# Attention's last column group computes keys first; the conformer's end runs by token half, with half of its x update inside the section

## The reference, cut to what matters

```python
# attention: three mixers on one projection of 2464 columns
proj = rmsnorm(x, ln1_g) @ w_in
qa, ka, va, cq, ckv, kr, qc, kc, vc = jnp.split(proj, split_idx, axis=-1)
out_a = mixer_dilated(qa, ka, va, ...)      # 6 heads of 64, rotary on q and k
out_b = mixer_mla(cq, ckv, kr, ...)         # 6 heads of 96
out_c = mixer_diff(qc, kc, vc, ...)         # 4 heads, two softmax maps each
x = x + jnp.concatenate([out_a, out_b, out_c], -1) @ w_o

# conformer, then x = x + rms_norm(result, g)
h = x @ w_pw1 + b_pw1
a, gate = jnp.split(h, 2, axis=-1)
h = causal_depthwise_conv(a * sigmoid(gate), w_dw) + b_dw    # 31 taps
h = silu(layernorm(h) * ln_g + ln_b)
return h @ w_pw2 + b_pw2
```

## Time and profile before

| | us |
|---|---|
| median of 3 runs | 1992.95 |
| profiled execution | 1992.19 |
| its span | 1990.4 |
| PE busy | 1945.3 (98% of the span) |
| DVE busy | 1285.6 (65%) |
| ACT busy | 970.8 (49%) |
| POOL busy | 87.0 (4%) |

### The profile page before, as it was taken

One profiled execution on the slowest core, in us unless ns is written; L12 is line 12 of the kernel. 1 busy time (PEld: TensorE's weight loads), 2 busy tenths in 40 slices (PEclk: granted clock), 3 DMA queues, 4 the chain that ended last, 5 costly groups with the idle time before them and its releaser, 6 DMA issues.

```text
span 1990.4 us, 26010 instructions
## 1 busy us (share of the span) xinstructions
PE 1945.3 (98%) x10642; PEld 1636.2 (82%) x10642; DVE 1285.6 (65%) x1649; ACT 970.8 (49%) x1251; POOL 87.0 (4%) x124
## 2 busy tenths in 40 slices
PE   6999999999999999999999999999999999999998
PEld 5768888868888887888888688889988888788887
DVE  5876565876655675676665476566765667557564
ACT  5645444655443544454455554444544453445443
POOL 0300000120000000001000000000000000000000
PEclk9999999999999999999999999999999999999999
DMA  7335654425654653566543356636566555445661
GB/s 251 127 101 175 190 190 144 170 85 185 194 191 160 222 189 127 165 202 193 191 144 120 115 187 195 191 128 210 181 211 190 190 201 190 158 154 182 190 190 63
DMA packets 197150, 340.61 MB, mean 171 GB/s; under 512 B 6757, under 2 KB 128233, under 8 KB 197032
## 3 DMA queue, kind: packets, MB, share of 16 engines
q1 hardware_dynamic: 193024, 331.04, 51.0%
q10 hardware_dynamic: 4008, 7.90, 1.2%
HBM read 337.88 MB, written 1.05 MB: 170 GB/s over the span
## 4 chain that ended last, share of the span: by engine, by line
PE 90%; DVE 6%; ACT 3%; issue 1%; DMA 0%; POOL 0%; DVEq 0%; ACTq 0%
PE ps L550 20%; PE ps L552 20%; PE ps L551 19%; PE ps L665 14%; PE ps L663 8%; PE ps L662 2%; PE ps L1066 1%; PE ps L572 1%; DVE arena L1920 1%; PE ps L1012 1%; PE ps L807 1%; PE ps L806 1%; ACT xT L1210 0%; DMA first_g<-ln_g_dram 0%; ACT arena L1359 0%
## 5 line engine op out<-in xcount | busy, mean ns | idle before, releaser
L1663 DVE TENSOR_TENSOR w_lo<-w_raw,w_hi 128x2048 fp32r<-128x2048 f32 x300 | 691.9, 2312 | 255.3 <-ACT w_hi L1158 254.8
L1158 ACT ACTIVATE w_hi<-w_raw 128x2048 fp32r<-128x2048 f32 x302 | 575.6, 1912 | 96.6 <-PE ps L552 86.2
L665 PE MATMUL ps<-xT,w_hi 128*128 128x512 f32 x1176 | 419.5, 396 | 0.0
L550 PE MATMUL ps<-w_hi,u_h 128*128 128x512 f32 (+1 forms) x1032 | 405.0, 392 | 3.9 <-DVE u_l L2124 1.8
L552 PE MATMUL ps<-w_hi,u_l 128*128 128x512 f32 (+1 forms) x1032 | 399.8, 387 | 0.0
L551 PE MATMUL ps<-w_lo,u_h 128*128 128x512 f32 (+1 forms) x1032 | 399.6, 387 | 0.0
L663 PE MATMUL ps<-xT,w_lo 128*128 128x256 f32 x1344 | 347.4, 279 | 0.0
L550 PE MATMUL ps<-w_hi,xT 128*128 128x512 f32 (+2 forms) x800 | 290.2, 363 | 9.4 <-DVE w_lo L1663 5.1
L552 PE MATMUL ps<-w_hi,xT 128*128 128x512 f32 (+2 forms) x800 | 284.2, 355 | 0.0
L551 PE MATMUL ps<-w_lo,xT 128*128 128x512 f32 (+2 forms) x800 | 284.0, 355 | 0.0
L663 PEld LDWEIGHTS ps<-xT,w_lo 128*128 128x128 f32 x1344 | 253.4, 189 | 13.6
(11 more groups left out here) (226 smaller groups left out, 1848.2 us busy)
## 6 DMA issues: line engine op xcount, KB each, us to landing
w_raw<-mlp_w_dram SPq DMA_DIRECT2D x128, 1024.0 KB, 5.4
w_raw<-ret_w_in_dram SPq DMA_DIRECT2D x48, 1024.0 KB, 5.1
w_raw<-w_up_dram SPq DMA_DIRECT2D x32, 1024.0 KB, 5.6
w_raw<-w_down_dram SPq DMA_DIRECT2D x32, 1024.0 KB, 4.8
w_raw<-w_in_dram SPq DMA_DIRECT2D x16, 1024.0 KB, 5.3
w_raw<-ret_w_out_dram SPq DMA_DIRECT2D x16, 1024.0 KB, 4.8
w_raw<-cf_w_pw_dram SPq DMA_DIRECT2D x12, 1024.0 KB, 5.4
w_raw<-sc_w_in_dram SPq DMA_DIRECT2D x12, 1024.0 KB, 5.2
```

The source lines that it names most:

```text
L550: pe.matmul(dst, lh, rh, start=start, stop=False)
L665: ins = pe.matmul(ps[:, bank, :], w_hi[:, slot, wsl], both, start=False, stop=kc == KC - 1)
L1158: act.activation(w_hi[:, slot, :], w_raw[:, slot, :], ACT.Copy).then_inc(hi_ready[slot], 1)
L1663: tt(w_lo[:, slot, :], w_raw[:, slot, :], w_hi[:, slot, :].bitcast(F32), ALU.subtract).then_inc(lo_ready[slot], 1)
```

## The change

In attention the second group's fillers (stages 8 to 15) are turned round: `late_chunk` multiplies the 256 key columns over all 8 row blocks in stages 8 to 11, two blocks a stage, then the 256 value columns in stages 12 to 15. Keys are taken out of PSUM in stage 11, values in stage 15. DVE rotates the first group in stages 9 and 10 (POOL no longer does) and the late keys in stage 14. `LATE` and its empty stage go; there are 24 stages. `out_chunk` takes token half 0 first. The splitting of one tile moves by one stage.

In the conformer up(tile 3) goes ahead of conv 0 and up(tile 5) ahead of conv 2, and the 7 `keep_busy` go. Conv 6 and 7 run as two token halves each. Everything behind them runs for half 0 and then half 1; `keep_busy` there runs 3 and 2 times. ACT has one silu of a single column ahead of the norm. The x update of half 0 (`add`, `sum_added`) is inside the section, the splitting of tiles 9 + 3 and 10 + 3 behind it, and `feed_x` of half 0 stands ahead of the last step of half 1.

```diff
-STAGES, LATE = MAPS + 5, 16
+STAGES, TURN_C = MAPS + 4, 15
...
+                def late_chunk(i):
+
+                    for kc in (2 * (i % 4), 2 * (i % 4) + 1):
+                        c, first = LATE_TILE + kc // 4, kc % 4 * 512 + 256 * (i // 4)
+                        slot = tile_ready(sec, c)
+                        for t in range(NT):
+                            ins = wide_part(sec, c, t, kc, 256, slice(first, first + 256), 2 * (i // 4) + t, 0, kc == 0, kc == KC - 1)
+                        if i >= 4 and kc % 4 == 3:
+                            ins.then_inc(used[slot], 1)
+                        elif i == 3 and kc == KC - 1:
+                            ins.then_inc(late_k.sem, 1)
...
                     if k == 0 and cc == 0:
-                        n = 4 if t == 1 else 5
+                        n = 5 + t
                         pe.wait_ge(evac_a.sem, evac_a.at(sec, n))
...
+                        if s == 12:
+                            pe.wait_ge(evac_a.sem, evac_a.at(sec, 4))
+                            pe.wait_ge(evac_v.sem, evac_v.at(sec, 4))
+                        late_chunk(s - 8)
...
-                def conv(c):
+                def conv(c, tok=slice(0, S)):
+                    bank = c % 4 - tok.start // 64
                     if c == 0:
-                        keep_busy(3, 7)
...
+                def back_late(t):
+                    for c in range(4, KC):
+                        ins = back(c, t)
+                    ins.then_inc(conv_T.sem, 1)
...
                 up(sec, 6, 2, lambda: turn_ups(sec, 1, cwide, lambda: pe.wait_ge(wu_sb.sem, wu_sb.at(sec, 2))))
+                up(sec, 7, 3)
                 conv(0)
                 conv(1)
-                up(sec, 7, 3)
                 pe.wait_ge(glu_done.sem, glu_done.at(sec, 1))
                 up(sec, 4, 4)
+                up(sec, 5, 5)
                 conv(2)
                 conv(3)
-                up(sec, 5, 5)
                 pe.wait_ge(glu_done.sem, glu_done.at(sec, 2))
                 up(sec, 6, 6)
...
+                conv(6, slice(0, P))
+                conv(7, slice(0, P))
+                conv(6, slice(P, S))
+                pe.wait_ge(conv_a.sem, conv_a.at(sec, 8))
+                back_late(0)
+                conv(7, slice(P, S))
+                pe.wait_ge(conv_a.sem, conv_a.at(sec, 10))
+                back_late(1)
...
+                def out_half(t, k):
+
+                    slot = tile_ready(sec, 8 + k)
+                    pe.wait_ge(feed_lo.sem, feed_lo.at(sec, 4 * t + k + 1))
+                    if t == 1 and k == 3:
+                        then(False)
+                    for cc in range(2):
+                        lh, ll = half_step(u_h, k)[:, cc, :], half_step(u_l, k)[:, cc, :]
...
+                keep_busy(0, 3)
+                pe.wait_ge(y_normed.sem, y_normed.at(sec, 1))
+                for k in range(4):
+                    turn_half(0, k)
+                keep_busy(0, 2)
+                out_half(0, 0)
+                out_half(0, 1)
                 pe.wait_ge(y_normed.sem, y_normed.at(sec, 2))
                 for k in range(4):
-                    if k >= 2:
-                        pe.wait_ge(feed_lo.sem, feed_lo.at(sec, k - 1))
-                    turn_step(sec, k, ch, k)
-                    if k == 1:
-                        keep_busy(3, 2)
-                    if 1 <= k < 3:
-                        down(sec, k - 1, 7 + k, first=k == 1)
-                last_downs(sec, 2, 10, then, True)
+                    turn_half(1, k)
+                out_half(0, 2)
+                out_half(0, 3)
+                for k in range(4):
+                    out_half(1, k)
+                then(True)
 
             def sc(prev, sec, then):
...
+                    if s == 11:
+                        act.wait_ge(late_k.sem, late_k.at(sec, 1))
+                        act.activation(pr[:, 0, 512:VA], ps[:, 0, 0:256], ACT.Copy, scale=rstd[:, 0:1]).then_inc(evac_a.sem, 1)
+                    if s == 15:
+                        act.wait_ge(used[sec.slot(LATE_TILE + 1)], sec.fill(LATE_TILE + 1) + 1)
+                        act.activation(pr[:, 0, VA:1024], ps[:, 2, 0:256], ACT.Copy, scale=rstd[:, 0:1]).then_inc(evac_a.sem, 1)
...
+                def high(t, k):
+                    n = 4 * t + k
+                    act.wait_ge(feed_T.sem, feed_T.at(sec, n + 3 if k < 2 else n + 1))
+                    if t == 1:
+                        act.wait_ge(feed_lo.sem, feed_lo.at(sec, k + 1))
...
+                    if t == 1 and k < 3:
+                        act.wait_ge(out_first.sem, out_first.at(sec, k + 1))
+                    elif t == 1:
+                        act.wait_ge(acc_ready.sem, acc_ready.at(sec, 2))
+                    act.activation(half_step(u_h, k), half_step(csl, k), ACT.Copy).then_inc(feed_hi.sem, 1)
+
+                act.activation(st[:, 8:9], mhalf[:, 0:1], ACT.Silu)
+                norm(0)
+                high(0, 0)
+                high(0, 1)
+                norm(1)
+                high(0, 2)
+                high(0, 3)
+                for k in range(3):
+                    high(1, k)
+                sum_added(sec, 0)
+                high(1, 3)
+                prepare(sec, 9)
+                prepare(sec, 10)
 
...
-                pool.wait_ge(rope_b.sem, rope_b.at(sec, 1))
-                pool.wait_ge(evac_a.sem, evac_a.at(sec, 4))
-                pool.wait_ge(evac_v.sem, evac_v.at(sec, 4))
-                for t in range(NT):
-                    ins = rotate(pool, step, pr[:, t, 0:512].rearrange("p (h d) -> p h d", d=AD), 512 // AD, AD // 2,
-                                 rope[:, t, 0:32], rope[:, t, 32:64], rope_pa, rope_pb)
...
+                    if s in (9, 10):
+                        t = s - 9
+                        vec.wait_ge(evac_a.sem, evac_a.at(sec, 4))
+                        vec.wait_ge(evac_v.sem, evac_v.at(sec, 4))
+                        ins = rotate(vec, step, pr[:, t, 0:512].rearrange("p (h d) -> p h d", d=AD), 512 // AD, AD // 2,
+                                     c64[t], s64[t], rope_va, rope_vb)
...
+                    if s == 14:
...
+                def low(t, k):
+                    vec.wait_ge(feed_hi.sem, feed_hi.at(sec, 4 * t + k + 1))
+                    tt(half_step(u_l, k), half_step(csl, k), half_step(u_h, k).bitcast(F32), ALU.subtract).then_inc(feed_lo.sem, 1)
+
+                statistics(0)
+                shift(0)
+                statistics(1)
+                low(0, 0)
+                shift(1)
+                for k in range(1, 4):
+                    low(0, k)
+                for k in range(3):
+                    low(1, k)
                 vec.wait_ge(bias_in.sem, bias_in.at(sec, 16))
+                add(sec, 0)
+                low(1, 3)
+                prepare(sec, 9)
+                prepare(sec, 10)
```

More of the change, by code:

```diff
@@ L930, in attn @@
                             values_pair(e)
-                    if turn and s == LATE + 1:
-                        turn_block(map_at(s))
                     filler(s)
@@ L1092, in cf @@
                 ins.then_inc(conv_T.sem, 1)
-                conv(6)
-                conv(7)
-                pe.wait_ge(conv_a.sem, conv_a.at(sec, KC))
-                for t in range(NT):
-                    for c in range(4, KC):
-                        ins = back(c, t)
-                    ins.then_inc(conv_T.sem, 1)
-                keep_busy(0, 8)
+                conv(6, slice(0, P))
+                conv(7, slice(0, P))
+                conv(6, slice(P, S))
+                pe.wait_ge(conv_a.sem, conv_a.at(sec, 8))
@@ new lines, in out_half @@
+                def out_half(t, k):
[5 more added lines that the diff above has]
+                        lh, ll = half_step(u_h, k)[:, cc, :], half_step(u_l, k)[:, cc, :]
+                        for h in range(2):
+                            wsl = slice(cc * D + h * 512, cc * D + h * 512 + 512)
+                            ins = three(ps[:, 2 * t + h, :], lh, ll, w_hi[:, slot, wsl], w_lo[:, slot, wsl],
+                                        k == 0 and cc == 0, k == 3 and cc == 1)
+                            if k == 3 and cc == 1 and not (t == 1 and h == 1):
+                                ins.then_inc(acc_ready.sem, 1)
+                    if t == 1:
+                        ins.then_inc(used[slot], 1)
+                    elif k < 3:
+                        ins.then_inc(out_first.sem, 1)
@@ L1439, in cf, with conv_out @@
             def cf(prev, sec):
-                def conv_out(c):
-                    act.wait_ge(conv_e.sem, conv_e.at(sec, c + 1))
-                    act.activation(ccv[:, c, :], ps[:, c % 4, 0:S], ACT.Identity, bias=gain("bdw", 0, c)).then_inc(conv_a.sem, 1)
+                def conv_out(c, n, tok=slice(0, S)):
+                    act.wait_ge(conv_e.sem, conv_e.at(sec, n))
```

(13 more changed lines are left out.)

121 lines of the change are left out of this document (59 added, 62 removed).

## The result

The changed kernel takes 1977.34 us, the median of four runs (1976.71 to 1978.84). The kernel before took 1992.76 in the runs beside it (1992.49 to 1993.24). The ratio is 0.9925, with a 95% interval of 0.9913 to 0.9937: 15.4 us faster. The forecast was 1981.0 us: 11.8 us off the profiled execution's 1992.19, and 0.76 more for the step from that execution to the median. The profiled execution after has a span of 1975.4 us, 15.0 shorter, and a mean granted clock of 1.000 where it was 0.998.

A forecast was written before the change was run, and what follows sets the result against it. PE bounds the kernel (busy 1945.3 of 1990.4 us), so only its idle time, half clock and empty work can be won. 4.8 + 2.4 + 1.4 + 3.2 = 11.8 us off 1992.19, plus 0.76 to the median: 1981.0, range 1976 to 1988.

The forecast's parts named there:

- Attention, PE's own work: Attention: 48 matmuls of 512 columns become 96 of 256 per layer, costing +0.5 us per layer, ends 0 and +1.
- POOL off: Attention, ninth stage: without POOL's contention DVE's maxima come 2.3 us earlier and PE's 1.64 us wait goes.
- DVE's new load: Attention: DVE's own rotations (4.2 us) and late keys (2.6) give back PE's early gain; map 16's scores start at 117.2.
- Attention, the sum: Attention: 2.8 us won in the first layer, 1.3 in the second; 3.2 taken for both, ends -3 and +6.
- The half clock: First attention, behind the late rotation: PE at 1.2 GHz for most of 120 to 123 us, about 1.5 us lost.
- The two filled waits: Conformer, ahead of conv 0 and conv 2: up(tile 3) and up(tile 5) fill waits, 4.8 us won, ends 3.9 and 4.8.
- The section's middle: Conformer, conv 6 to first output matmul: token halves take 14.1 us against 16.56, 2.4 us won.
- The x update: Conformer's end: half 0's update hides behind remaining output matmuls, the 1.18 wait goes; 1.4 us won, ends 0 and 1.9.
- (a): Conformer rival: weight loads set the floor, so a 128-token conv instruction costs what 256 tokens do; 1987 us, chance 0.10.
- (b): Attention rival: DVE is the bound throughout, PE waits 2 us more per layer, clock falls once; 1986.5 us, chance 0.15.
- (c): Conformer rival: half convs' loads run one after another at 110 ns, +20 us; 2001 us, chance 0.04.
- (d): Better case: half convs cost exactly half and attention keeps no wait but DVE's last; 1977 us, chance 0.06.

The follow-up runs named there:

- rot_only: The kernel before with DVE instead of POOL rotating columns 0 to 511 in stages 9 and 10, empty stage and late rotation kept; 1988.71 us.
- attn_pool: The kernel before with the attention part of the change, but POOL still rotating columns 0 to 511; 1990.55 us.
- dve_order: The changed kernel with DVE's sub-head norm (stage 13) and values' evacuation (stage 15) put ahead of low parts that wait for ACT; 1975.26 us.
- fill_only: The kernel before with only up(tile 3) ahead of conv 0 in place of `keep_busy` and up(tile 5) ahead of conv 2; 1987.47 us.
- no_early_silu: The changed kernel without the single-column silu that loads ACT's table ahead of the norm; 1976.67 us.
- best: The changed kernel with `dve_order`'s DVE order, the single-column silu behind conv 5's copy, and one multiplication instead of three in the first `keep_busy`; 1973.01 us.
- no_keep_busy: The changed kernel without the five `keep_busy` multiplications between the convolutions and the output product; 1979.59 us.

## Why the prediction was right, step by step

The direction and the size were right: forecast 1981.0 with 1976 to 1988, measured 1977.34. It is 3.7 us lower than the forecast, 2.5 of it in attention and 1.1 in the conformer, worked out from the places of PE above. It lies below the likeliest case's own range, 1978 to 1985. The terms did not cancel: attention, the middle and the x update each gave more than forecast (2.5, 0.4 and 0.9), the filled waits 0.1 less.

**Attention, PE's own work.** Forecast +0.5 us per layer. A stage's filler now takes 1.51 to 1.53 us where it took 1.47 to 1.49: 0.04 in each of eight, 0.3 per layer. Right in kind, but it was subtracted at the wrong place, as the paragraph on the sum shows.

**POOL off.** Right in mechanism and place: 0.23 and 0.75 are back, the wait at the ninth stage is gone. By `rot_only` and `attn_pool` it is the larger part of attention's gain, 3.8 to 3.9 us, of which in `rot_only` 1.4 is the cheaper fall of the clock.

**DVE's new load: the reading that failed.** The walk gave the scores of map 16 at 117.2, and they came at 117.0 on that scale. It also said that "all that PE gained at 93 is given back by then, in small waits of 0.2 to 0.9 us". By map 15 that is so, 0.22 us are left of 1.71. But the cause was to be DVE's own rotations, and `attn_pool` shows the same loss and the same waits without the 4.2 us of them. Work that DVE takes up in stages 9 and 10 does not reach PE; DVE's total of 26.4 us was no chain on which PE depends throughout. So that the place came out to 0.2 us is in part luck. What the late keys' rotation costs, 2.6 of the 6.8 us, no run separates. `dve_order` gives 2.1 us back without any work taken off DVE. Of the idle time that I counted on, 3.2 us per layer, 1.7 is there.

**Attention, the sum.** From map 16's scores on the forecast was 6.05 us won there less 2.7 of work put off; the traces have 6.23 and 3.61 at the second turning of x, so 2.62. Then I took off 0.5 for the narrower matmuls. That was an error: they all lie ahead of map 16's scores, whose place the walk had set by DVE, so their cost was already in it. This makes 2.8 of what became 3.6 in the first layer, and 1.3 of what became 2.1 in the second. Last, I took 3.2 us for both layers, towards the lower account, instead of 4.1; by the traces it is 5.7. These two choices, 1.0 and 0.9, are most of the 2.5 us that attention gave beyond the forecast.

**The half clock.** In the profiled execution the fall at 120 us did not come back, in either layer. I had priced it at 1.5 and the two layers of the kernel before give 1.53. But the fall is not the same in every execution, even of one kernel: of 47 runs of the kernel before beside the experiments, 28 have a mean clock of 0.998 and a median of 1992.6 us, and 19 one of 0.999 or 1.000 and a median of 1990.8. Of the changed kernel's four runs the one with 0.998 is the slowest, 1978.84. That it fell in other kernels with waits of 0.4 and 0.65 us at the same places as in the changed one, in which it did not, is not explained by these runs.

**The two filled waits.** 4.8 forecast, 4.67 in the trace, 4.6 for `fill_only`. Nothing was late behind them.

**The section's middle.** Forecast 14.1 us, 2.4 less; measured 13.79, 2.77 less. Of its two parts, the one to the end of the first half's transposes took 5.96 where 6.6 was forecast, the rest 7.83 where it was 7.5, so two misses partly cancel. The half convolution was taken at 0.032 us an instruction. From 1092.80 to 1098.18 there are 192: 0.028 each, half of the 0.0555 that one of 256 tokens took. The table load ahead of the norm was forecast as a delay of 1.5; by `no_early_silu` it is 1.40 (9.77 less 8.37). Its price at PE is less, 0.88.

**The x update.** Forecast 1.4, measured 2.29 from the first output matmul to the second turning of x (30.61 before, 28.32 after). The wait of 1.18 is gone, as forecast. The second half's wait went from 0.74 to 0.18, which I had left where it was: 0.56. Most of the other 0.55 lies around the first of these waits: from the last product ahead of the turning to the second product behind it PE takes 2.96 us before (1140.18 to 1143.14) and 1.33 after (1126.38 to 1127.71), 1.63 less where the wait's own figure is 1.18. With a wait, the eight transposes are 1.07 us from their start to the next product, without it 0.79.

**The rivals.** (a), that the weight load sets the floor, is refuted by the 0.028: four strips that differ in columns alone run at half the time for half the tokens, and no load is exposed. The statement of the Trainium skill, "TensorE: Matmul & The Clock Gate", "Part 3: Packing small matmuls — row/col tiling", that loads overlap running matmuls only where the row group differs, is not borne out by this trace. (c), slower by loads one after another, is refuted by the same rows. (b), DVE as the bound throughout, is refuted by the waits, 1.7 us a layer and not the 5.2 of this rival, and by `attn_pool`; it holds for single stages, as `dve_order` shows. (d), 1977 with halves that cost exactly half and no wait but DVE's last, gave the time to 0.3 us; its first condition is met, its second is not, since three waits a layer are left.

**The warning on the clock.** I had written that I would be wrong if the clock fell in the conformer, where `keep_busy` was thinned. It did not fall with five multiplications, and `best` shows that three are enough here. It fell with none. So that step was sound, and not by a wide margin.

## What to carry to other kernels

When a stage waits for an engine, find the operation in that engine's queue that itself waits, and ask whether ready work stands behind it: here two blocks put in front of it gave 2.1 us, and no sum of the engine's busy time would have found them. Before an engine's work is added up into a chain, ask at how many places the other engine meets it. Where a place is set by one engine's chain, what the other engine does ahead of it must not be subtracted once more. When waits are cut up or multiplications that only fill time are thinned, read the granted clock of the next few microseconds, since it is there that the price is paid, unless PE would have waited further on anyway.

## What the hardware showed that I had not expected

- Four column strips of a matmul with 32-column weight loads run at 0.028 us for 128 tokens and 0.0555 for 256, although one load lasts 0.110 us, before as after.
- In `no_early_silu` ACT's table load at 1101.91 runs before the input of its activation is there (wait of 0.18 us behind it, at 1103.37). So where the engine would be idle anyway, leaving the load where it falls costs less than calling for it early: 12.91 against 13.79 us in the middle.
- A stretch at 1.2 GHz with the same shortfall of the clock, 1.7 us, cost 1.53, 0.78 and 0.13 us in three kernels: the less, the longer PE would have waited for another engine behind it.
- In `no_keep_busy` a wait of 1.96 us and one of 1.47 behind it cost 2.29 us by the clock alone; with three multiplications in them (`best`) the granted clock stays at 1.000.
